# Three inner sums of a Strassen-form MLP stored as high and low parts in the up phase

## The reference, cut to what matters

```python
x = x + gate1 * mixed                                   # x1: attention and retention, projected
h = rms_norm(x, norm2_g) * (1.0 + scale2) + shift2
x = x + gate2 * (jnp.square(jax.nn.relu(h @ w_mlp1)) @ w_mlp2)
```

## Time and profile before

| | |
|---|---|
| time, median of 3 runs | 1139.66 us (1139.42 to 1140.14) |
| profiled execution | 1139.11 us, of which the span 1137.3 |
| mean granted TensorE clock | 0.985 |
| PE busy | 1093.8 us (96%) |
| DVE busy | 762.2 us (67%) |
| ACT busy | 442.0 us (39%) |
| POOL busy | 244.0 us (21%) |
| DMA of SP's queue | 122.45 MB, 33.4% of 16 engines' span |
| h_spill, stores and loads | 64 stores of 256 to 768 KB, 28 loads of 1024 KB |

### The profile page before, as it was taken

How to read it: one execution, slowest core, us unless ns; L and a number is a source line. 1 busy time by engine, 2 the same in 40 slices (tenths; PEclk the granted TensorE clock), 3 DMA queues, 4 the chain that set the end, 5 groups by cost and what they waited for, 6 DMA issues and landing times. The chain is left out here.

```text
span 1137.3 us, 14052 instructions
## 1 busy us (share of the span) xinstructions
PE 1093.8 (96%) x5210; PEld 884.9 (78%) x5210; DVE 762.2 (67%) x1206; ACT 442.0 (39%) x746; POOL 244.0 (21%) x219
## 2 busy tenths in 40 slices
PE   5999999999999999997999999999899999999998
PEld 4578877777778988775888888888678788787786
DVE  5673556564546767897676767667986957848752
ACT  6342333354444334662232323233523514426231
POOL 2011000000001105312222323233323223232231
PEclk9899999999999999998999999999999999999999
DMA  9958433332013013103535353537626345336205
GB/s 272 275 163 265 130 123 101 122 101 90 28 38 122 28 33 108 38 0 130 193 113 191 114 190 116 187 120 224 257 95 233 135 148 191 99 117 222 74 1 148
DMA packets 150932, 151.71 MB, mean 133 GB/s; under 512 B 14116, under 2 KB 124880, under 8 KB 147280
## 3 DMA queue, kind: packets, MB, share of 16 engines
q1 hardware_dynamic: 142800, 122.45, 33.4%
q0 software_dynamic: 8064, 28.36, 7.6%
HBM read 113.04 MB, written 37.75 MB: 133 GB/s over the span
## 5 line engine op out<-in xcount | busy, mean ns | idle before, releaser
L739 PE MATMUL ps<-cmb_hi,wm_hi 128*128 128x512 f32 x880 | 350.0, 398 | 23.2 <-DVE wm_lo L1904 8.1
L740 PE MATMUL ps<-cmb_lo,wm_hi 128*128 128x512 f32 x880 | 346.2, 393 | 0.0
L741 PE MATMUL ps<-cmb_hi,wm_lo 128*128 128x512 f32 x880 | 346.1, 393 | 0.0
L739 PEld LDWEIGHTS ps<-cmb_hi,wm_hi 128*128 128x128 f32 x880 | 167.6, 190 | 65.7 <-issue 12.4
L741 PEld LDWEIGHTS ps<-cmb_hi,wm_lo 128*128 128x128 f32 x880 | 167.4, 190 | 35.7
L740 PEld LDWEIGHTS ps<-cmb_lo,wm_hi 128*128 128x128 f32 x880 | 167.7, 191 | 34.6 <-issue 0.5
L739 PE MATMUL ps<-act_hi,w_hi 128*128 128x512 f32 x400 | 162.3, 406 | 3.0 <-DVE act_lo L1682 3.0
L740 PE MATMUL ps<-act_lo,w_hi 128*128 128x512 f32 x400 | 157.1, 393 | 0.0
L741 PE MATMUL ps<-act_hi,w_lo 128*128 128x512 f32 x400 | 157.0, 392 | 0.0
L1392 ACT ACTIVATE wm_hi<-wm_f 128x512 fp32r<-128x512 f32 x128 | 77.2, 627 | 204.7 <-POOL wm_f L709 158.0
L2155 DVE SCALAR_TENSOR_TENSOR x1t<-ps,ada,x1t 128x512 f32<-128x512 f32 x112 | 83.5, 746 | 79.8 <-PE ps L741 79.8
(11 more groups left out here) (200 smaller groups left out, 1406.4 us busy)
## 6 DMA issues: line engine op xcount, KB each, us to landing
raw<-in_w_mlp_dram SPq DMA_DIRECT2D x128, 256.0 KB, 3.9
cmb_f<-h_spill SPq DMA_DIRECT2D x22, 1024.0 KB, 5.3
wada<-in_w_ada_dram POOLq DMA_DIRECT2D x32, 512.0 KB, 5.0
h_spill<-stage SPq DMA_DIRECT2D x16, 768.0 KB, 6.5
w_raw<-in_w_in_dram SPq DMA_DIRECT2D x18, 512.0 KB, 3.9
ada_rows<-in_w_ada_dram SPq DMA_DIRECT2D x16, 512.0 KB, 7.3
h_spill<-stage SPq DMA_DIRECT2D x32, 256.0 KB, 3.2
h_spill<-stage SPq DMA_DIRECT2D x16, 512.0 KB, 6.7
```

The source lines that it names most:

```text
L739: pe.matmul(bank, wh, hi, start=first, stop=False, skip_group_check=onto)
L740: pe.matmul(bank, wh, lo, start=False, stop=False, skip_group_check=onto)
L741: return pe.matmul(bank, wl, hi, start=False, stop=last, skip_group_check=onto)
```

## The change

T1, T2 and T3 are no longer stored in float32 and split at each chunk start. In the up phase ACT copies the three sums of a pair to a high part in one instruction (`hidden_hi`), DVE subtracts to get the low part in one instruction, in place of the sums in the stage (`hidden_lo`), and SP stores both (`t_spill`, twice 768 KB a pair). The down phase loads T1, T2 and T3 as two loads of 1 MB each straight into the operands' places, and PE waits for the loads. The memory for the high parts and for b12 is that of the x1 tiles 6 and 7. SP writes these two to DRAM (1 MB) before the up phase's loop and reads them back in down pair 17. b21 and NT4 are now stored ahead of the sums, and the order on ACT and DVE changes in the first pairs and at the chunk starts.

The core of the diff (semaphore declarations, the renamed b12 operand and the counting tables are left out):

```diff
-FIRST_LOADS = (B11, B21, T1, T2, T3, B22, NT4)
-STORED = (B11, B22, T1, T2, T3, B21, NT4)
+STORED = (B11, B22, B21, NT4)
+STORED_SPLIT = (T1, T2, T3)
+PIECES = (B11, B21, B22, NT4)
...
+        sums_low = at("sums_low", [3, HALF], TMPB + 6 * KB, F32R)
+        sums_high = at("sums_high", [3, HALF], REG + 24 * KB, F32R)
+        b12 = at("b12", [HALF], REG + 30 * KB)
...
@@ SP @@
+            def store_split(p, sem_done, ready, dst, src):
+                q, j = divmod(p, CHUNK_PAIRS)
+                sp.wait_ge(ready, p + 1)
+                sp.dma_start(t_spill[q, dst, :, j, :].rearrange("i p n -> p i n"), src[:, :, :].bitcast(F32)).then_inc(sem_done, 16)
+
             def store_sums(p):
-                sp.wait_ge(s_tt, 4 * p + 3)
-                store(p, s_stt, slice(2, 5), slice(ST_T1, ST_T3 + 1))
+                store_split(p, s_sth, s_hth, slice(0, 3), sums_high)
+                store_split(p, s_stl, s_htl, slice(3, 6), sums_low)
...
             def load_in_place(q, i):
                 sp.wait_ge(s_pd, PRODUCT[PAIRS - 1 + CHUNK_PAIRS * q, i])
-                load_combination(q, i, cmb_f[i])
+                if i in STORED_SPLIT:
+                    n = STORED_SPLIT.index(i)
+                    sp.dma_start(cmb_hi[i][:, :, :].bitcast(F32), t_spill[q, n]).then_inc(s_cl[i], 16)
+                    sp.dma_start(cmb_lo[i][:, :, :].bitcast(F32), t_spill[q, 3 + n]).then_inc(s_cl[i], 16)
+                else:
+                    load_combination(q, i, cmb_f[i])
...
+            sp.wait_ge(s_evb, 2 * N_OUT)
+            sp.dma_start(x_spill[KT - 2:KT].rearrange("k p n -> p k n"), x1t[:, KT - 2:KT, :]).then_inc(s_x1out, 16)
+
             for p in range(PAIRS):
+                if p == PAIRS - 1:
+                    load_in_place(0, T1)
                 sp.wait_ge(s_wlm, SPLIT[p, A22])
                 load_pair(p + 2)
+                if p == PAIRS - 1:
+                    load_in_place(0, T3)
                 if p:
+                    store_b21(p - 1)
                     store_sums(p - 1)
-                    store_b21(p - 1)
...
                 if p == 1:
+                    store_b22(1)
                     store_b11(1)
+                    store_b11(2)
+                    continue
...
-            for i in FIRST_LOADS[2:]:
+            for i in (T2, B22, NT4):
                 load_in_place(0, i)
...
                 if w == PAIRS + 1:
                     store_b22(PAIRS - 1)
+                    store_b21(PAIRS - 1)
                     store_sums(PAIRS - 1)
-                    store_b21(PAIRS - 1)
+                    sp.wait_ge(s_sth, 16 * PAIRS)
+                    sp.dma_start(x1t[:, KT - 2:KT, :], x_spill[KT - 2:KT].rearrange("k p n -> p k n")).then_inc(s_x1in, 16)
@@ ACT @@
+            def hidden_hi(p):
+                act.wait_ge(s_tt, 4 * p + 3)
+                if p == 0:
+                    act.wait_ge(s_h2, 2 * KT)
+                    act.wait_ge(s_x1out, 16)
+                wait(act, s_sth, 16 * p)
+                act.activation(sums_high[:, :, :], stage[:, ST_T1:ST_T3 + 1, :], ACT.Copy).then_inc(s_hth, 1)
...
                 if p == 1:
                     weight_hi(1, A22)
                     e5(1)
-                    e2(1)
-                    e1(2)
+                    hidden_hi(0)
                 elif p:
                     weight_hi(p, A22)
                     if p + 1 < PAIRS:
                         e1(p + 1)
+                    hidden_hi(p - 1)
                     e5(p)
                 if p and p + 1 < PAIRS:
                     weight_hi(p + 2, A11)
                     weight_hi(p + 2, A12)
                 weight_hi(p + 1, S3)
                 weight_hi(p + 1, S1)
-                if p >= 2:
+                if p:
                     e2(p)
-                if p == PAIRS - 1:
-                    combination_hi(0, T1)
+                if p == 1:
+                    e1(2)
                 weight_hi(p + 1, S2)
@@ DVE @@
+            def hidden_lo(p):
+                dve.wait_ge(s_hth, p + 1)
+                dve.wait_ge(s_tt, 4 * p + 4)
+                dve.tensor_tensor(sums_low[:, :, :], stage[:, ST_T1:ST_T3 + 1, :], sums_high[:, :, :].bitcast(F32),
+                                  ALU.subtract).then_inc(s_htl, 1)
```

More of the change, by code:

```diff
@@ L87 @@
 UP_COPIES = [("e1", 0), ("e1", 1), ("e5", 0), ("e2", 0), ("e5", 1), ("e2", 1), ("e1", 2)]
-UP_SUMS = [("e25", 0), ("c22", 0), ("c11", 1), ("c11", 0), ("c12", 0), ("e25", 1), ("c22", 1), ("c21", 0), ("c11", 2),
-           ("c12", 1), ("c21", 1)]
-SQUARES = [("b22", 0), ("b11", 0), ("b12", 0), ("b21", 0), ("b11", 1), ("b11", 2), ("b22", 1), ("b12", 1)]
+UP_SUMS = [("e25", 0), ("c22", 0), ("c11", 1), ("c11", 0), ("c12", 0), ("e25", 1), ("c22", 1), ("c21", 0), ("c12", 1),
+           ("c21", 1), ("c11", 2)]
+SQUARES = [("b22", 0), ("b11", 0), ("b12", 0), ("b21", 0), ("b22", 1), ("b11", 1), ("b12", 1), ("b11", 2)]
 for _p in range(2, PAIRS):
@@ L429, in hybrid_layer @@
         ST_B22, ST_T1, ST_T2, ST_T3, ST_B21, ST_NT4 = 2, 3, 4, 5, 6, 7
-        def loads_of(q):
-            return FIRST_LOADS if q == 0 else tuple(range(7))
+        B12 = "b12"
         def piece(q, i, part):
-            return 14 * q + 2 * loads_of(q).index(i) + part + 1
+            return 8 * q + 2 * PIECES.index(i) + part + 1
         def halves_of(part):
@@ L1560, in _ @@
                     weight_hi(w + 1, S3)
-                if ends:
-                    combination_hi(q + 1, T2)
-                if more:
                     weight_hi(w + 1, S1)
@@ L1568, in _ @@
                     weight_hi(w + 1, S2)
-                if ends:
-                    combination_hi(q + 1, T1)
-                if more:
                     weight_hi(w + 1, S4)
+                if w == PAIRS + 1:
+                    hidden_hi(PAIRS - 1)
             for i, (m, half, bank) in enumerate(((6, 0, TURN_BANK), (7, 1, TURN_BANK + 1), (6, 1, LAST_BANK),
@@ L2075, in _ @@
             c11(0)
+            weight_lo(1, S1)
             c12(0)
@@ L2086, in _ @@
             c22(1)
+            weight_lo(3, A11)
+            weight_lo(3, A12)
             c21(0)
@@ L2089, in _ @@
             last_sum(0)
+            squared(ST_B22, n_c22(1))
             squared(1, n_c11(1))
+            weight_lo(2, S3)
+            weight_lo(2, S1)
+            hidden_lo(0)
+            c12(1)
+            squared(B12, n_c12(1))
+            weight_lo(2, S2)
+            c21(1)
             c11(2)
             squared(0, n_c11(2))
[L2093 to L2101 removed]
             for p in range(2, PAIRS):
                 weight_lo(p, S4)
+                if p == PAIRS - 1:
+                    both_lo(0, B11)
                 weight_lo(p, A22)
@@ L2183, in _ @@
                 add_product(w, 2)
-                if w == PAIRS:
-                    weight_lo(w, S4)
-                    weight_lo(w, A22)
-                elif pp == 0:
+                if pp == 0:
                     combination_lo(q, B22, 1)
-                    weight_lo(w + 1, A12)
+                    if w == PAIRS:
+                        weight_lo(w, S4)
+                        weight_lo(w, A22)
+                    combination_lo(q, NT4, 0)
                 elif ends:
@@ L2195, in _ @@
                 add_product(w, 3)
-                if w == PAIRS:
-                    both_lo(0, B22)
-                elif pp == 0:
-                    both_lo(q, NT4)
+                if pp == 0:
+                    combination_lo(q, NT4, 1)
+                    weight_lo(w + 1, A11)
                 elif w == PAIRS + 1:
@@ L2231, in _ @@
                     weight_lo(w + 1, S2)
+                if w == PAIRS + 1:
+                    next(remains)
 _INS = ["x", "c", "norm1_g", "norm2_g", "w_ada", "b_ada", "w_in", "q_norm_g", "k_norm_g", "sinks", "ret_norm_g",
```

90 lines of the change are left out of this document (34 added, 56 removed).

## The result

The changed kernel takes 1160.53 us (median of 4 runs, 1157.74 to 1163.49) against 1139.54 for the kernel before, measured beside it: a ratio of 1.0181 [1.0154, 1.0209]. Forecast were 1143.5 us and a range of 1135 to 1150. So it is slower, as forecast, but by 21 us where I had 4, and outside the range. The profiled execution took 1158.29 us, its span 1156.5 against 1137.3: 19.2 us to account for.

A forecast was written before the change was run, and what follows sets the result against it. PE, busy 96% of the span, was taken to bound the kernel. From 1139.1 us, A +2.5, B +1.4, C +4.9, D +3.3 and E -7.7 sum to +4.4: 1143.5 us, range 1135 to 1150.

The forecast's parts named there:

- E: Starts of down chunks 2 to 4: PE loses 1.5 plus 0.2 us instead of 4.3, 3 x -2.6 = -7.7 us.
- C: First down chunk: T2 lands about 815 behind a full queue, PE stands 8.9 us; net +4.9 us.
- B: Pairs 1 to 3: the 9.5 us lost now are lost in three smaller waits, +1.4 us in all.
- A: Start of the up phase: the copy of x1 tiles 6 and 7 delays pair 2's weights, +2.5 us.
- that supposes the full clock: Condition of E at chunk starts: PE's wait of 1.5 us leaves the clock up.
- the 2.1 us that PE loses next now, on B22's and NT4's splits, go: Step of C, after pair 16's fourth product: this 2.1 us loss vanishes, turning +7.0 into +4.9 us.
- R1: Rival, faster: pairs 1 to 3 run freely, -9.4 us in place of +1.4, 1132.7 us; 20% with its like in C.
- D: Pair 17 to 18: hidden_lo(15) ahead of an addition makes PE's wait 2.45 us and brings the low clock, +3.3 us.
- R3: Rival, much slower: at chunk starts B22 lands 1 us later, clock falls, 3 x -0.5 us, 1149.8 us; 15%.

The follow-up runs named there:

- experiment 11: Changed kernel with b22(1), b11(1) stored ahead of pair 0's low part and two of DVE's sums in pair 2 ahead of pair 4's weight splits: 1156.16 us.
- Experiments 1 to 3: Changed kernel, chunk starts: B22 loaded before T3, 1158.78 us; also A11's split behind the fifth addition, 1159.42; whole order on queue, ACT and DVE, 1153.05.
- Experiments 5 and 6: Changed kernel, first down chunk's queue: T2's load third, 1160.51 us; whole chunk start order plus queue in order of use, 1143.32 us.
- 14 and 15: ACT's last copy in the last up pair put ahead of hidden_hi(14): in the kernel of experiment 13, 1131.43 us; in the changed kernel alone, 1162.90 us.
- experiment 13: Changed kernel with chunk start and first-chunk queue orders, hidden_lo(0) earlier, x1 copy and hidden_lo(15) later, plus both edits of experiment 11: 1129.92 us.
- experiment 4: Changed kernel with the copy of x1 tiles 6 and 7 behind load_pair(2) in SP's order: 1158.51 us.
- experiment 8: Changed kernel with hidden_lo(15) three slots later, behind the first addition of pair 18: 1160.53 us.

## Why the prediction was wrong, step by step

*Direction and places: right.* All the loss lies in stretches where I had forecast a change, and nothing else moved: eleven up pairs at 19.04, and E's steady pairs too. Of the 14.8 us missed in the profiled execution (19.2 against 4.4), 7.7 are E, 4.7 C, 2.8 B and 0.8 A, less 1.2 by which the front was shorter.

*E, -7.7, measured 0.0: the step that failed.* The landing was right. This is the DMA view of the issues of T3's and B22's loads at chunk 3 (count, KB, us to landing); T2's went out first, at 972.48, B22's at 980.64:
```profile
cmb_hi<-t_spill SPq DMA_DIRECT2D x1, 1024.0 KB, 9.4
cmb_lo<-t_spill SPq DMA_DIRECT2D x1, 1024.0 KB, 11.5
cmb_f<-h_spill SPq DMA_DIRECT2D x1, 1024.0 KB, 11.6
```
B22 landed at 992.2, 19.8 us after T2's issue; forecast was 974, 20.2 behind T2's issue of 953.8 in the kernel before. That was in part luck: the 3.15 MB more are ahead of NT4, and B22 comes 1.05 MB sooner, so my own numbers give 968.9 + 2.1/0.42 = 973.9 for its last byte and not 972.9, and the queue made up for it with 422 to 430 GB/s from 976 to 990. PE's first wait there was 1.11 at the full clock (chunk 2: 1.80, and the clock fell), about my 1.5. Wrong was to stop at that addition. DVE's timeline, as it goes on:
```profile
993.38 1.23 DVE L2073 TENSOR_TENSOR cmb_lo<-cmb_f,cmb_hi 128x1024 fp32r<-128x1024 f32 x1 [3.82 <-ACT cmb_hi L1521]
994.52 0.75 DVE L2201 SCALAR_TENSOR_TENSOR x1t<-ps,ada,x1t 128x512 f32<-128x512 f32 x1
995.18 2.78 DVE L2073 TENSOR_TENSOR cmb_lo<-cmb_f,cmb_hi 128x1024 fp32r<-128x1024 f32 x2
997.88 0.74 DVE L2201 SCALAR_TENSOR_TENSOR x1t<-ps,ada,x1t 128x512 f32<-128x512 f32 x1
998.54 2.25 DVE L2073 TENSOR_TENSOR cmb_lo<-cmb_f,cmb_hi 128x1024 fp32r<-128x1024 f32 x1
1000.71 1.77 DVE L1936 TENSOR_TENSOR wm_lo<-raw,wm_hi 128x512 fp32r<-128x512 f32 x1
1002.41 0.74 DVE L2201 SCALAR_TENSOR_TENSOR x1t<-ps,ada,x1t 128x512 f32<-128x512 f32 x1
```
Three additions (L2201), each behind splits: B22's first half; its second and NT4's first; NT4's second and A11. Each frees the PSUM bank that PE wants next, so the second and third cost 0.34 and 1.51 more. The last two splits took 2.25 and 1.77 where 1.21 and 0.68 are usual, 2.1 us more, because POOL's weight sums ran at that moment. At chunk 4 the same collision hit B22's first half (2.14), the wait was 3.15 and the clock fell. At chunk 2 one wait and the low clock are all that PE's timeline shows, but the rest of the chain is there too: in experiment 11, with the same code there, the clock stayed up, the further waits appear, and the start took 23.52 against 22.74:
```profile
914.79 0.50 PE L772 MATMUL ps<-cmb_hi,wm_hi 128*128 128x512 f32 x1 [1.75 <-DVE x1t L2210]
918.14 0.50 PE L772 MATMUL ps<-cmb_hi,wm_hi 128*128 128x512 f32 x1 [0.33 <-DVE x1t L2210]
922.66 0.50 PE L772 MATMUL ps<-cmb_hi,wm_hi 128*128 128x512 f32 x1 [1.51 <-DVE x1t L2210]
```
So my other condition, "that supposes the full clock", failed at chunks 2 and 4, and at chunk 2 holding it would have gained nothing. I had counted what DVE loses (3 x 2 splits) and not that the rest of its queue now starts when B22 lands. Experiments 1 to 3 show it in order: the landing alone gives 2.9 us, with A11's place 6.0, with each split behind the addition that it used to delay 8.3, where the forecast was 7.7.

*C, +4.9, measured +9.6.* The mechanism held: a wait of 9.44 for T2 (forecast 8.9), T2's halves landing 11.0 and 12.2 us after their issue. Its fourth product ended 2.3 us later than forecast, counted from number 15: T2 landed 1.5 later, and the clock was low for longer. The queue moved 371 GB/s from 795 to 823 us; my sum had 9.45 MB in 24.75 us, 382 GB/s. That accounts for about half of the 1.5; the other half stays open. The other 2.4 is the step "the 2.1 us that PE loses next now, on B22's and NT4's splits, go". They stayed, 21.47 where before had 21.14, by E's mechanism: PE waited 0.45 and 1.37 us for additions (L2201) that stand behind NT4's halves and A11(17), and these splits, too, took about 1 us more each while POOL was at work. DVE's timeline:
```profile
831.57 2.32 DVE L2073 TENSOR_TENSOR cmb_lo<-cmb_f,cmb_hi 128x1024 fp32r<-128x1024 f32 x1
833.81 0.74 DVE L2201 SCALAR_TENSOR_TENSOR x1t<-ps,ada,x1t 128x512 f32<-128x512 f32 x1
834.47 2.12 DVE L2073 TENSOR_TENSOR cmb_lo<-cmb_f,cmb_hi 128x1024 fp32r<-128x1024 f32 x1
836.51 1.78 DVE L1936 TENSOR_TENSOR wm_lo<-raw,wm_hi 128x512 fp32r<-128x512 f32 x1
838.21 0.74 DVE L2201 SCALAR_TENSOR_TENSOR x1t<-ps,ada,x1t 128x512 f32<-128x512 f32 x1
```
Experiments 5 and 6 confirm that the queue's order is the cause of T2's wait (C -3.3 and, with the chunk start's order, -6.7, of which the queue's part is 4.7), 14 and 15 that ACT's part is not.

*B, +1.4, measured +4.2, and 6.8 to 8.2 in six other kernels with the same code there* (62.7 to 64.0 against 55.83; experiments 5 and 6 had 60.1 and 61.1). The chain was the right one, each link later: load_pair(3) was issued at 525.26 and its data came at 531.3 where I had 520.8 and 527.6. A explains 2.2 of that; the rest is the splits of S2(1) and S4(1), which took 3.44 us together in place of 1.28, again with POOL at work. hidden_lo(0) ended at 539.4 (535.7), e1(2) began at 544.93 (540.5), e5(2) at 554.20 (548.9). From number 1 to 3 PE lost 15.3 us against 13 undisturbed products. The three waits that I had forecast (2.92, 4.91, 0.62) are 11.8 of them with the low clock, where I had about 11. The rest is a wait of 1.32 for A11(3), for which my chain had next to nothing, and one of 2.20 for S2(1), which with the 1.39 for S1(1) that went makes +0.5 where I had -0.3. R1 was right that this stretch could run faster than before, but not in this order of the code: 51.81 in experiment 13, a measured -4.0 against the -9.4 that I gave R1. I had bounded B by +3.

*A, +2.5, measured +3.3,* inside its bounds of 1 to 4; taken away whole by experiment 4. *D, +3.3, measured +3.3,* wait and clock both (2.43 and 0.58); taken away by experiment 8.

*R3* had E's outcome, "the chunk starts give nothing", by another mechanism (B22 1 us late, clock down); it had 15%. The range failed because each term's bounds were drawn around one chain with all later links on time, and these errors have one sign: E missed wholly, B and C for the most part, by what stood beside or behind the wait that I had priced.

*What stays open.* The changed kernel's four runs lie near 1158 and near 1163. B alone varies by 4 us and the front by as much between profiled executions, which is enough for it; no run here shows which of them makes the two groups. Why B takes 60 us in one profile and 64 in another is open too, and with it what each repair in B gives alone. In E no run separates DVE's order from ACT's.

## What to carry to other kernels

When a change takes a late thing away, follow the in-order queue behind it to its end: price each later instruction that frees a buffer with everything that now stands ahead of it, not the first wait alone. Look first at what stands between the additions, since here the work removed gave nothing in the chunk starts (0.0 us) until the order was changed too (-8.3). Judge an edit by its stretch of the trace, against more than one profile of the kernel without it: B of the unchanged code varied by 4 us, as much as most single repairs gave. And measure the combination before rejecting any of them: moving hidden_lo(0) alone left a wait of 4.41 us, the two other edits alone one of 4.91, and all three left neither. A stretch is also only as good as its mark: POOL's starts told PE's progress until an edit made POOL wait for a load instead.
